# Latent attention heads: two banks in turn for the sums of values, and a ring of three banks for the rest

## The chip, the cores and the metric

One Trainium2 chip, one of its cores. The metric is the device time of the core in microseconds (us), median of several runs. The engines that matter here are TensorE (PE: matmuls, which write to PSUM alone), ScalarE (ACT), VectorE (DVE) and GpSimd (POOL). PSUM is the memory between them: 8 banks of 512 float32 values in each of 128 partitions.

## What is computed

Two layers of a hybrid backbone over 512 latent tokens and 256 context tokens, width 1024. Each layer has neighbourhood attention (4 heads), a bidirectional mLSTM (4 heads), latent attention (8 heads of 64 + 32 query and key features, 64 value features), an output projection for each, and a SwiGLU feed-forward part. The change lies in latent attention:

```python
def attend(q, k, v, scale):
    s = jnp.einsum('bqhd,bkhd->bhqk', q, k).astype(jnp.float32) * scale
    p = jax.nn.softmax(s, axis=-1).astype(v.dtype)
    return jnp.einsum('bhqk,bkhd->bqhd', p, v)

def mla_project(p, gq, gkv, w_uq, w_ukv, qk_gain, rope):
    B, T, _ = p[8].shape
    q = (rms_norm(p[8], gq) @ w_uq).reshape(B, T, MLA_HEADS, MLA_NOPE + MLA_ROPE)
    kv = (rms_norm(p[9], gkv) @ w_ukv).reshape(B, T, MLA_HEADS, MLA_NOPE + MLA_V)
    k_nope, v = kv[..., :MLA_NOPE], kv[..., MLA_NOPE:]
    k_rope = jnp.broadcast_to(p[10][:, :, None, :], (B, T, MLA_HEADS, MLA_ROPE))
    q = rms_norm(q, qk_gain[0])
    k = rms_norm(jnp.concatenate([k_nope, k_rope], axis=-1), qk_gain[1])
    if rope is not None:
        ...
    return q, k, v

# in each of the DEPTH layers, behind neighbourhood attention and the mLSTM:
qc_l, kc_l, vc_l = mla_project(pl, mla_gq[l], mla_gkv[l], w_uq[l], w_ukv[l], mla_qk_gain[l], rope)
qc_c, kc_c, vc_c = mla_project(pc, mla_gq[l], mla_gkv[l], w_uq[l], w_ukv[l], mla_qk_gain[l], None)
oc_l = blocked_attention(qc_l, jnp.concatenate([kc_l, kc_c], axis=1),
                         jnp.concatenate([vc_l, vc_c], axis=1), MLA_SCALE)
...
if need_ctx:
    oc_c = attend(qc_c, kc_c, vc_c, MLA_SCALE)
```

In layer 0 the context tokens are needed too (their queries attend to context keys alone); in layer 1, the last, they are keys and values but no queries.

## The kernel before, in words

Every engine runs its own hand-written program, and semaphores tie them together. Each float32 operand is split into a high part (fp32r) and a remainder, and a product is three matmuls (`mm3`, L877): high with high, high with low, low with high. GpSimd makes the low parts of the weights, which stream in by DMA from SyncE.

The latent heads of a layer are software-pipelined in `latent_pe` (L1224), `latent_act` (L692) and `latent_dve` (L1842). All three loop over h from -2 to 8, and inside over steps i (7 in layer 0, 6 in layer 1; `lat_steps`). While head h is scored, head h + 1 gets its scales, its rounded queries and keys and its column maxima, head h + 2 its projections, and head h - 1 its output. In one step TensorE runs, in this order:

- `scores(h, i)`: keys of tile i against all latent queries into a bank ("st"); step 6 of layer 0 is the context's own scores. ScalarE takes the exponential of it (L708) and so frees the bank; VectorE splits that into high part (L1864) and remainder (L1865).
- at i = 0, `q_sums`: sums of squares of the queries of h + 1 ("sumq"), read by ScalarE's Ln (L738).
- at i = 2, `k_project` of h + 2, then at i = 2 and 3 (in layer 0 once more at 5) `max_context`: scores of context keys for maxima ("ctx"), reduced by VectorE (L1901), at i = 3 `q_project` of h + 2; at i = 3, 4, 4, 5 `max_scores` ("max"), reduced by VectorE (L1896).
- at i = 4, `k_sums` of h + 2 ("sumk"), read by ScalarE's Ln (L729), which it does at i = 5, behind the exponential of step 5.
- `values` of the step two places back: values with a column of ones against the probabilities, summed over six steps in bank `AV_BANK` (7). In layer 0 a seventh step writes the context's sums into a ring bank ("avc").
- at the last step, `max_row` ("row"): the maxima of h + 1 turned into a row, which ScalarE copies (L754). Score step 0 of the next head waits for that copy.

The projections Q_PS and K_PS hold banks 3 to 5 (bank 4 is shared). Banks 0, 1, 2 and 6 form a ring: `ring_order` (L309) writes down the order of all fills of both layers once, and `fill` (L1228) has TensorE wait until the bank of fill number `at` was released by the reader of fill `at - 4`. A fill's reader is found with `filled`. Each fill is released by one instruction of ScalarE or VectorE.

The output of head h - 1 is made at step 2 of head h: ScalarE's `q_round` of h + 1, then `inverse(h - 1, 0)` (Ln L767, Exp L768) of the sums in `AV_BANK`, VectorE's product L1917 (`o_scale(h - 1, 0)`), then in layer 0 `inverse(h - 1, 1)`, which waits for L1917, and the product L1920 (`o_scale(h - 1, 1)`), whose drain releases "avc". Behind these VectorE has, in order, `k_rest` (L1887), `q_rest` (L1891), `probs_lo(h, 2)`, and at step 3 `max_c` twice (L1901), `o_rest` (L1928) and `probs_lo(h, 3)`. The first step of values of head h waits for L1917 of head h - 1, since both use `AV_BANK`:

```python
if i == 0 and o_count(l, h, 0):
    pe.wait_ge(o_mul, o_count(l, h, 0) - (1 if full and h else 0))
```

Names below: "st3" is the fill of score step 3, "ctx0" that of `max_context(h + 1, 0)`, "max0" of `max_scores(h + 1, 0)`, and so on. "Head 2" is the stretch from the start of score step 0 of h = 2 to that of h = 3.

Of the kernel before, what the change touches and what calls it, by code (L numbers as in the profile page):

```python
# [70 lines left out]
def build(nc, x_t, c_t, w_mod, w_stream, cols, rpb, c_f32, c_rope, c_gate, c_dir, out):  # L71
# [3 lines left out]
    with es:  # L75
# [268 lines left out]
            return (2 * h if l < DEPTH - 1 else MLA_HEADS * (DEPTH - 1) * 2 + h) + x  # L344

        RINGS = ring_order()
        RING_BANKS = (0, 1, 2, 6)
        K_PS = psum[:, 512 * 4 + 256:512 * 6]
        Q_PS = psum[:, 512 * 3:512 * 3 + TOK]
        AV_BANK = 7  # L350
        XQ, CQ = slice(0, SEQ), slice(SEQ, TOK)

        def o_rows(h):
# [97 lines left out]
        def _(act):  # L451
# [240 lines left out]
            def latent_act(l, full):  # L692
# [4 lines left out]

                def filled(*name):
                    at = RINGS[(l,) + name]
                    act.wait_ge(bank_full[at % 4], at // 4 + 1)  # L700
                    return bank(RING_BANKS[at % 4]), at % 4

                def probs(h, i):
                    s = lat_step(l, h, i)
# [19 lines left out]
                def k_rsqrt(h):  # L724
                    if G(h):
                        act.wait_ge(k_lo, G(h))
                    for x, (c0, c1) in enumerate(((CTX_LEN, TOK), (0, CTX_LEN))):
                        src, b = filled("sumk", h, x)
                        A(rk[:, c0:c1], src[:, 0:c1 - c0], ACT.Ln, bias=eps[:, 0:1], scale=1.0 / QK_DIM).then_inc(bank_free[b], 1)  # L729
                    act.wait_ge(bank_free[b], RINGS[l, "sumk", h, 1] // 4 + 1)  # L730
                    A(rk, rk, ACT.Exp, scale=-0.5).then_inc(k_r, 1)

                def q_rsqrt(h):
                    if G(h):
                        act.wait_ge(q_lo, G(h))
                    for x, cs in enumerate((XQ, CQ) if full else (XQ,)):
                        src, b = filled("sumq", h, x)
                        A(rq[:, cs], src[:, 0:cs.stop - cs.start], ACT.Ln, bias=eps[:, 0:1],  # L738
                          scale=1.0 / QK_DIM).then_inc(bank_free[b], 1)
                    act.wait_ge(bank_free[b], RINGS[l, "sumq", h, 1 if full else 0] // 4 + 1)  # L740
                    A(rq[:, 0:qw], rq[:, 0:qw], ACT.Exp, scale=-0.5).then_inc(q_r, 1)

                def k_round(h):
# [12 lines left out]
                def inverse(h, x):  # L756
                    ro, rs = o_rows(h)
                    cs = (XQ, CQ)[x]
                    if x == 0:
                        act.wait_ge(av_x, lat_x(l, h, TT - 1))  # L760
                        src = bank(AV_BANK)
                    else:
                        src, b = filled("avc", h)
                    m = o_count(l, h, x)
                    if m:
                        act.wait_ge(o_mul, m)
                    seq(A(MA["rec"][ro, cs], src[rs, 0:cs.stop - cs.start], ACT.Ln))  # L767
                    A(MA["rec"][ro, cs], MA["rec"][ro, cs], ACT.Exp, scale=-1.0).then_inc(o_rec, 1)  # L768
# [98 lines left out]
        def _(pe):  # L867
# [356 lines left out]
            def latent_pe(l, full):  # L1224
# [3 lines left out]
                def fill(*name):  # L1228
                    at = RINGS[(l,) + name]
                    assert at == nfill[0]  # L1230
                    nfill[0] += 1
                    if at >= 4:
                        pe.wait_ge(bank_free[at % 4], at // 4)
                    return bank(RING_BANKS[at % 4]), at % 4

                def scores(h, i):
                    dst, b = fill("st", h, i)
                    sl = h % 2
                    kh, kl, qh, ql = (MA[x][0:97, sl, :] for x in ("khi", "klo", "qhi", "qlo"))
                    if i == 0:  # L1240
                        pe.wait_ge(k_lo, G(h) + 1)
                        pe.wait_ge(q_lo, G(h) + 1)
                        at = RINGS[l, "row", h, 0]
                        pe.wait_ge(bank_free[at % 4], at // 4 + 1)
                    if i < TT:
                        ks = slice(P * i, P * i + P)
                        ins = mm3(dst, kh[:, ks], kl[:, ks], qh[:, XQ], ql[:, XQ], True, True)
                    else:
                        at = RINGS[l, "row", h, 1]
                        pe.wait_ge(bank_free[at % 4], at // 4 + 1)  # L1250
                        for k in range(CT):
                            ks = slice(P * k, P * k + P)
                            ins = mm3(dst[:, CTX_LEN * k:CTX_LEN * k + CTX_LEN], kh[:, ks], kl[:, ks],
                                      qh[:, CQ], ql[:, CQ], True, True)
                    ins.then_inc(bank_full[b], 1)

                def values(h, i):
                    s = lat_step(l, h, i)
                    pe.wait_ge(p_lo, s + 1)
                    if i < TT:  # L1260
                        if i == 0 and o_count(l, h, 0):
                            pe.wait_ge(o_mul, o_count(l, h, 0) - (1 if full and h else 0))
                        mm3(bank(AV_BANK), v_ones(hhi, h, i), v_ones(hlo, h, i), MA["phi"][:, s % 3, :],
                            MA["plo"][:, s % 3, :], i == 0, i == TT - 1).then_inc(av_x, 1)
                    else:
                        dst, b = fill("avc", h)
                        for k in range(CT):
                            cs = slice(CTX_LEN * k, CTX_LEN * k + CTX_LEN)
                            ins = mm3(dst[:, 0:CTX_LEN], v_ones(hhi, h, k), v_ones(hlo, h, k), MA["phi"][:, s % 3, cs],
                                      MA["plo"][:, s % 3, cs], k == 0, k == CT - 1)  # L1270
                        ins.then_inc(bank_full[b], 1)
# [190 lines left out]
        def _(dve):  # L1462
# [379 lines left out]
            def latent_dve(l, full):  # L1842
# [4 lines left out]

                def filled(*name):
                    at = RINGS[(l,) + name]
                    dve.wait_ge(bank_full[at % 4], at // 4 + 1)  # L1850
                    return bank(RING_BANKS[at % 4]), at % 4

                def probs_lo(h, i):
                    s = lat_step(l, h, i)
                    at = RINGS[l, "st", h, i]
                    dve.wait_ge(bank_free[at % 4], at // 4 + 1)
                    back = lat_back(l, h, i, 3)
                    if back is not None:
                        if back[1] < TT:
                            dve.wait_ge(av_x, lat_x(l, *back))  # L1860
                        else:
                            at = RINGS[l, "avc", back[0]]
                            dve.wait_ge(bank_full[at % 4], at // 4 + 1)
                    seq(V.tensor_copy(MA["phi"][:, s % 3, :], MA["p"][:, s % 2, :]))  # L1864
                    V.tensor_tensor(MA["plo"][:, s % 3, :], MA["p"][:, s % 2, :], MA["phi"][:, s % 3, :],  # L1865
                                    ALU.subtract).then_inc(p_lo, 1)

                def v_lo(t):
                    at = RINGS[l, "v", t]
                    dve.wait_ge(ma_v, TT * l + t + 1)  # L1870
                    v = bank(RING_BANKS[at % 4]).rearrange("p (j a n) -> p j a n", j=MLA_HEADS // 2, a=2)
                    V.tensor_tensor(v_heads(hlo, t, 0), v[:, :, 0, :], v_heads(hhi, t, 0), ALU.subtract)
                    V.tensor_tensor(v_heads(hlo, t, 1), v[:, :, 1, :], v_heads(hhi, t, 1), ALU.subtract).then_inc(bank_free[at % 4], 1)

                def k_scale(h):
                    dve.wait_ge(k_r, G(h) + 1)
# [26 lines left out]

                def max_both(h):
                    at = RINGS[l, "max", h, 3]
                    dve.wait_ge(bank_free[at % 4], at // 4 + 1)
                    V.tensor_tensor(mx[:, 8:12], mx[:, 0:4], mx[:, 4:8], ALU.max).then_inc(col_max, 1)

                def o_scale(h, x):
                    ro, rs = o_rows(h)  # L1910
                    cs = (XQ, CQ)[x]
                    m = o_count(l, h, x)
                    dve.wait_ge(o_rec, m + 1)
                    if x == 0:
                        if m:
                            dve.wait_ge(o_hi, m)
                        V.tensor_tensor(MA["of"][ro, cs], bank(AV_BANK)[ro, :], MA["rec"][ro, cs], ALU.mult).then_inc(o_mul, 1)  # L1917
                    else:
                        at = RINGS[l, "avc", h]
                        seq(V.tensor_tensor(MA["of"][ro, cs], bank(RING_BANKS[at % 4])[ro, 0:CTX_LEN], MA["rec"][ro, cs], ALU.mult))  # L1920
                        V.drain().then_inc(bank_free[at % 4], 1)
                        V.drain().then_inc(o_mul, 1)

                def o_rest(h, x):
# [285 lines left out]
```

## Time and profile before

| what | value |
|---|---|
| median of 3 runs | 2615.68 us (2615.37 to 2619.78) |
| the profiled execution, its time | 2617.63 us |
| the profiled execution, its span | 2615.9 us |
| mean granted clock of TensorE | 0.895 of full speed |
| latent heads of layer 0, first score to the end of the last head (640.97 to 853.00) | 212.0 us, TensorE busy 178.1 |
| latent heads of layer 1 (2029.88 to 2203.00) | 173.1 us, TensorE busy 139.4 |

The page gives busy time per engine, the chain of work that ended last and the costliest groups of instructions. A group's "idle before" says how long its engine had nothing to do ahead of it and what ended the idle time. Timelines list instructions by start; PE's matmuls are pipelined, so a busy TensorE isn't one at its peak, and successive rows overlap. The granted clock is the share of full speed that TensorE was allowed.

### The profile page before, as it was taken

What the parts mean: (1) busy time and instruction counts of PE and PEld (TensorE: products, weight loads), DVE (VectorE), ACT (ScalarE), POOL (GpSimd) and SP (SyncE); (2) the same over time, 40 slices, a digit from 0 to 9 for tenths busy, and PEclk for the clock granted to TensorE, in tenths of its full rate; (3) what the DMA queues carried; (4) which work ended last, traced back from release to release, by engine and by line L of the source; (5) the groups of instructions that cost most, each with busy time, mean ns of one, the idle gap of its engine ahead of it and who ended that gap; (6) DMA issues with size and microseconds to landing.
All of it is one profiled execution on the core that took longest, in us unless ns stands there. A gap on an engine that the chain in (4) does not pass through costs nothing.

```text
span 2615.9 us, 29223 instructions
## 1 busy us (share of the span) xinstructions
PE 2231.0 (85%) x11572; PEld 1781.0 (68%) x11572; DVE 1017.7 (39%) x1774; ACT 723.8 (28%) x1178; POOL 615.6 (24%) x820
## 2 busy tenths in 40 slices
PE   5777999596887799999999967798766887899998
PEld 4466766474665688788878855686655555688886
DVE  4457501616777511111201155550334885311211
ACT  3233222023554311111111133322113553322222
POOL 0110300021000233333333320031021101455555
PEclk8899965698998799999999979997588998999999
DMA  6200124010000124132323210021011000232322
GB/s 244 89 15 10 55 81 145 1 58 24 9 9 9 56 97 129 60 118 97 105 73 129 81 43 17 17 63 33 0 43 33 17 9 18 79 97 97 96 90 97
DMA packets 76733, 166.23 MB, mean 64 GB/s; under 512 B 5296, under 2 KB 47024, under 8 KB 75584
## 3 DMA queue, kind: packets, MB, share of 16 engines
q1 hardware_dynamic: 75648, 163.15, 19.1%
q8 instruction: 92, 1.51, 0.2%
q10 hardware_dynamic: 960, 1.31, 0.2%
q14 instruction: 33, 0.27, 0.0%
HBM read 162.33 MB, written 2.10 MB: 63 GB/s over the span
## 4 chain that ended last, share of the span: by engine, by line
PE 73%; DVE 13%; ACT 6%; issue 5%; DMA 1%; POOL 1%; SPq 0%; DVEq 0%; ACTq 0%; POOLq 0%
PE psum L879 19%; PE psum L880 18%; PE psum L881 18%; PE psum L1133 2%; PE psum L924 2%; PE psum L1158 2%; DMA wm<-w_mod 1%; PE psum L934 1%; PE psum L1121 1%; PE psum L1316 1%; DVE naptlo L1627 1%; PE psum L1176 1%; PE psum L1187 1%; DVE n_t L1536 1%; PE psum L1031 1%
## 5 line engine op out<-in xcount | busy, mean ns | idle before, releaser
L441 POOL TENSOR_TENSOR wlo<-raw,whi 128x256 fp32r<-128x256 f32 x816 | 615.4, 786 | 1987.4 <-ACT whi L467 1987.4
L879 PE MATMUL psum<-hhi,whi 128*128 128x512 f32 (+1 forms) x1640 | 587.4, 358 | 46.0 <-DVEq L1474 14.6
L880 PE MATMUL psum<-hlo,whi 128*128 128x512 f32 (+1 forms) x1640 | 582.0, 355 | 0.0
L881 PE MATMUL psum<-hhi,wlo 128*128 128x512 f32 (+1 forms) x1640 | 581.1, 354 | 0.0
L467 ACT ACTIVATE whi<-raw 128x1024 fp32r<-128x1024 f32 x204 | 215.3, 1059 | 1060.8 <-PE psum L881 1060.6
L879 PEld LDWEIGHTS psum<-hhi,whi 128*128 128x128 f32 x1640 | 314.2, 192 | 102.2 <-issue 21.8
L881 PEld LDWEIGHTS psum<-hhi,wlo 128*128 128x128 f32 x1640 | 314.2, 192 | 42.7
L880 PEld LDWEIGHTS psum<-hlo,whi 128*128 128x128 f32 x1640 | 314.8, 192 | 40.6
L1983 DVE TENSOR_TENSOR ffuf<-ffsa,psum 128x768 f32<-128x768 f32 (+1 forms) x44 | 36.1, 821 | 534.2 <-ACT ffsa L828 534.2
L879 PE MATMUL psum<-uhi,whi 128*128 128x512 f32 (+1 forms) x528 | 190.9, 362 | 8.3 <-POOL wlo L441 7.5
L880 PE MATMUL psum<-ulo,whi 128*128 128x512 f32 (+1 forms) x528 | 189.6, 359 | 0.0
L881 PE MATMUL psum<-uhi,wlo 128*128 128x512 f32 (+1 forms) x528 | 189.3, 359 | 0.0
L1991 DVE SCALAR_TENSOR_TENSOR xres<-psum,mods,xres 128x512 f32<-128x512 f32 x72 | 45.4, 659 | 262.5 <-PE psum L881 262.5
L879 PEld LDWEIGHTS psum<-uhi,whi 128*128 128x128 f32 x528 | 100.0, 189 | 26.9 <-POOL wlo L441 9.2
L880 PEld LDWEIGHTS psum<-ulo,whi 128*128 128x128 f32 x528 | 100.6, 191 | 16.0
L881 PEld LDWEIGHTS psum<-uhi,wlo 128*128 128x128 f32 x528 | 100.0, 189 | 16.3
L1721 DVE TENSOR_TENSOR mle<-mle,psum 128x768 f32<-128x768 f32 x16 | 15.3, 955 | 228.3 <-ACT mle L648 172.2
L708 ACT ACTIVATE map<-psum 128x512 f32<-128x512 f32 x104 | 61.7, 595 | 136.8 <-PE psum L881 135.7
L1865 DVE TENSOR_TENSOR maplo<-map,maphi 128x512 fp32r<-128x512 f32 x104 | 75.4, 725 | 3.6
L879 PE MATMUL psum<-maphi,hhi 128*128 128x512 f32 (+1 forms) x112 | 53.7, 479 | 25.7 <-DVE maof L1917 24.1
L1553 DVE SCALAR_TENSOR_TENSOR xres<-psum,mods,xres 128x512 f32<-128x512 f32 x72 | 45.4, 659 | 70.2 <-PE psum L881 70.2
L924 PE MATMUL psum<-wm,csil 128*32 128x256 f32 x768 | 64.8, 465 | 3.3 <-DMA wm<-w_mod 3.3
(280 smaller groups left out, 3443.0 us busy)
## 6 DMA issues: line engine op xcount, KB each, us to landing
raw<-w_stream SPq DMA_DIRECT2D x204, 512.0 KB, 3.5
wm<-w_mod SPq DMA_DIRECT2D x80, 512.0 KB, 4.6
wm<-w_mod SPq DMA_DIRECT2D x8, 1024.0 KB, 17.3
xres<-x_t SPq DMA_DIRECT2D x8, 384.0 KB, 6.0
out<-xres SPq DMA_DIRECT2D x8, 256.0 KB, 2.9
mlsel<-c_gate ACTq DMA_DIRECT2D x2, 216.0 KB
consts<-c_f SPq DMA_DIRECT2D x1, 353.0 KB, 7.1
marope<-c_rope ACTq DMA_DIRECT2D x4, 64.0 KB
```

The source lines that it names most:

```text
L441: ins = nc.gpsimd.tensor_tensor(wlo[:, q % 2, c:c + UW // 4], raw[:, q % RAW, c:c + UW // 4], whi[:, q % 2, c:c + UW // 4], ALU.subtract)
L467: A(whi[:, q % 2, :], raw[:, q % RAW, :], ACT.Copy).then_inc(hi_done, 1)
L708: A(MA["p"][:, s % 2, :], src, ACT.Exp, scale=scale).then_inc(bank_free[b], 1)
L879: mm(dst, ah, bh, start=first, stop=False)
L880: mm(dst, ah, bl, start=False, stop=False)
L881: return mm(dst, al, bh, start=False, stop=last)
L924: ins = mm(dst[32 * j:32 * j + 32, 0:256], csil[:, 4 * half + j, :], w[:, j, :], start=half == 0, stop=half == 1)
L1133: mm(dst, sel[:, P * x:P * x + P], rows[:, 2, r0:r1], start=True, stop=False)
L1158: ins = mm(bank(4 + d)[:, 65 * c:65 * c + 65], e[:, d, P * c:P * c + P], va[:, c, h, :], start=True, stop=True)
L1553: ins = V.scalar_tensor_tensor(xres[:, m, r0:r1], psum_pair(psum, m % 4)[:, r0:r1], mods[:, l, 16 + m, cls(r0):cls(r0) + 1], xres[:, m, r0 ...
L1865: V.tensor_tensor(MA["plo"][:, s % 3, :], MA["p"][:, s % 2, :], MA["phi"][:, s % 3, :], ALU.subtract).then_inc(p_lo, 1)
L1991: ins = V.scalar_tensor_tensor(xres[:, m, r0:r1], psum_pair(psum, m % 2)[:, r0:r1], mods[:, l, 40 + m, cls(r0):cls(r0) + 1], xres[:, m, r0 ...
```

## The change

Bank 6 leaves the ring and becomes a second bank for the sums of values; even heads use bank 7, odd heads bank 6. The first step of values of head h waits for the product L1917 of head h - 2 instead of h - 1 (in layer 1 the heads 0 and 1 wait for the last output of layer 0). The ring has three banks: fill `at` waits for the release of fill `at - 3`. Every other place that named the ring's 4 names its length. The order of instructions on every engine is the same; line numbers behind L346 grow by one.

```diff
         RINGS = ring_order()
-        RING_BANKS = (0, 1, 2, 6)
+        RING_BANKS = (0, 1, 2)
+        NRB = len(RING_BANKS)
         K_PS = psum[:, 512 * 4 + 256:512 * 6]
         Q_PS = psum[:, 512 * 3:512 * 3 + TOK]
-        AV_BANK = 7
+        AV_BANKS = (7, 6)
...
                 def filled(*name):
                     at = RINGS[(l,) + name]
-                    act.wait_ge(bank_full[at % 4], at // 4 + 1)
-                    return bank(RING_BANKS[at % 4]), at % 4
+                    act.wait_ge(bank_full[at % NRB], at // NRB + 1)
+                    return bank(RING_BANKS[at % NRB]), at % NRB
...
                     if x == 0:
                         act.wait_ge(av_x, lat_x(l, h, TT - 1))
-                        src = bank(AV_BANK)
+                        src = bank(AV_BANKS[h % 2])
...
                     at = RINGS[(l,) + name]
                     assert at == nfill[0]
                     nfill[0] += 1
-                    if at >= 4:
-                        pe.wait_ge(bank_free[at % 4], at // 4)
-                    return bank(RING_BANKS[at % 4]), at % 4
+                    if at >= NRB:
+                        pe.wait_ge(bank_free[at % NRB], at // NRB)
+                    return bank(RING_BANKS[at % NRB]), at % NRB
...
                     if i < TT:
-                        if i == 0 and o_count(l, h, 0):
-                            pe.wait_ge(o_mul, o_count(l, h, 0) - (1 if full and h else 0))
-                        mm3(bank(AV_BANK), v_ones(hhi, h, i), v_ones(hlo, h, i), MA["phi"][:, s % 3, :],
+                        if i == 0 and (l or h >= 2):
+                            pe.wait_ge(o_mul, o_count(l, h - 2, 0) + 1 if h >= 2 else o_count(l, 0, 0))
+                        mm3(bank(AV_BANKS[h % 2]), v_ones(hhi, h, i), v_ones(hlo, h, i), MA["phi"][:, s % 3, :],
                             MA["plo"][:, s % 3, :], i == 0, i == TT - 1).then_inc(av_x, 1)
...
-                        V.tensor_tensor(MA["of"][ro, cs], bank(AV_BANK)[ro, :], MA["rec"][ro, cs], ALU.mult).then_inc(o_mul, 1)
+                        V.tensor_tensor(MA["of"][ro, cs], bank(AV_BANKS[h % 2])[ro, :], MA["rec"][ro, cs], ALU.mult).then_inc(o_mul, 1)
                     else:
                         at = RINGS[l, "avc", h]
-                        seq(V.tensor_tensor(MA["of"][ro, cs], bank(RING_BANKS[at % 4])[ro, 0:CTX_LEN], MA["rec"][ro, cs], ALU.mult))
-                        V.drain().then_inc(bank_free[at % 4], 1)
+                        seq(V.tensor_tensor(MA["of"][ro, cs], bank(RING_BANKS[at % NRB])[ro, 0:CTX_LEN], MA["rec"][ro, cs], ALU.mult))
+                        V.drain().then_inc(bank_free[at % NRB], 1)
                         V.drain().then_inc(o_mul, 1)
```

Left out: the same replacement of 4 by NRB in the other waits on bank_full and bank_free (ScalarE's Ln and Exp, TensorE's waits of `scores` for "row", VectorE's `filled`, `probs_lo`, `v_lo` and `max_both`), which wait for the same events as before.

## Rows read from the trace of the kernel before

**Rows 1.** The page, part 1: busy us, share of the span, instructions of each engine

```profile
PE 2231.0 (85%) x11572; PEld 1781.0 (68%) x11572; DVE 1017.7 (39%) x1774; ACT 723.8 (28%) x1178; POOL 615.6 (24%) x820
```

**Rows 2.** Waits of TensorE over the span: us in total, times, longest

```profile
PE psum L879 <- DVE maof L1917: 24.1, 14, 2.8
```

**Rows 3.** Stretches: one head each, then half-clock and full-clock ones; columns in the head row

```profile
core 0: us, PE busy (x) PEld busy (x) DVE busy (x) ACT busy (x) POOL busy (x), PEclk, DMA share, GB/s
693.50:720.62 27.12, 23.70 (x109) 17.35 (x109) 21.60 (x35) 15.80 (x27) 3.45 (x4) 0.94 0.06 19
2072.11:2094.17 22.06, 18.08 (x80) 12.74 (x80) 18.96 (x30) 12.60 (x20) 3.55 (x4) 1.00 0.08 25
2094.17:2117.03 22.86, 19.66 (x79) 14.00 (x80) 17.98 (x30) 11.57 (x20) 0.00 (x0) 0.93 0.00 1
703.68:707.09 3.41, 3.41 (x10) 2.74 (x11) 2.52 (x4) 1.35 (x4) 0.00 (x0) 0.50 0.00 0
707.10:710.80 3.70, 3.70 (x22) 3.19 (x21) 3.56 (x7) 1.14 (x2) 0.00 (x0) 1.00 0.00 0
```

**Rows 4.** Timeline, layer 0, head 2: start, duration, engine, line, operation [idle before]

```profile
703.53 0.63 PE L879 MATMUL psum<-maphi,hhi 128*128 128x512 f32 x1 [1.57 <-DVE maof L1917]
...
704.33 0.43 DVE L1920 TENSOR_TENSOR maof<-psum,marec 64x256 f32<-64x256 f32 x1 [0.95 <-ACT marec L768]
...
704.81 0.63 PE L879 MATMUL psum<-maqhi,makhi 97*128 97x512 f32 x1
...
706.51 0.63 PE L1327 MATMUL psum<-makhi,maqhi 96*128 96x512 f32 x1
...
707.91 1.29 DVE L1901 TENSOR_REDUCE mamax<-psum 128x2 f32<-128x512 f32 x2
...
710.84 0.40 PE L879 MATMUL psum<-maqhi,makhi 97*128 97x512 f32 x1
```

**Rows 5.** Timeline, the same head, from its score step 4 on

```profile
711.75 0.60 ACT L708 ACTIVATE map<-psum 128x512 f32<-128x512 f32 x1 [3.48 <-PE psum L881]
...
712.01 1.45 PE L1316 MATMUL psum<-masqk,consts 96*128 96x512 f32 x4
...
714.00 0.40 PE L879 MATMUL psum<-maqhi,makhi 97*128 97x512 f32 x1
...
715.02 0.68 DVE L1896 TENSOR_REDUCE mamax<-psum 128x1 f32<-128x512 f32 x1
715.52 1.05 ACT L729 ACTIVATE mar<-psum,eps 128x512 f32<-128x512 f32 x2
...
715.76 0.50 PE L1327 MATMUL psum<-makhi,maqhi 96*128 96x512 f32 x1 [0.89 <-DVE mamax L1896]
...
716.26 0.50 PE L1337 MATMUL psum<-makhi,maqhi 96*128 96x256 f32 x2
```

**Rows 6.** Timeline, layer 1: head 2 in two lines, then head 3

```profile
2083.16 0.39 PE L1327 MATMUL psum<-makhi,maqhi 96*128 96x512 f32 x1
...
2083.99 1.29 DVE L1901 TENSOR_REDUCE mamax<-psum 128x2 f32<-128x512 f32 x2
...
2105.45 0.68 DVE L1901 TENSOR_REDUCE mamax<-psum 128x2 f32<-128x512 f32 x1
...
2106.27 0.53 PE L1327 MATMUL psum<-makhi,maqhi 96*128 96x512 f32 x1
...
2113.66 0.40 PE L1327 MATMUL psum<-makhi,maqhi 96*128 96x512 f32 x1
...
2114.36 1.05 ACT L729 ACTIVATE mar<-psum,eps 128x512 f32<-128x512 f32 x2
...
2115.13 1.03 PE L1346 MATMUL psum<-consts,mamax 128*1 128x128 f32 x8 [0.37 <-ACT mar L729]
```

**Rows 7.** Timeline, layer 0, head 7, the last of the layer

```profile
834.50 0.42 DVE L1920 TENSOR_TENSOR maof<-psum,marec 64x256 f32<-64x256 f32 x1 [0.95 <-ACT marec L768]
...
837.67 0.63 PE L879 MATMUL psum<-maqhi,makhi 97*128 97x512 f32 x1
```

More of the change, by code:

```diff
@@ L729, in k_rsqrt @@
                         A(rk[:, c0:c1], src[:, 0:c1 - c0], ACT.Ln, bias=eps[:, 0:1], scale=1.0 / QK_DIM).then_inc(bank_free[b], 1)
-                    act.wait_ge(bank_free[b], RINGS[l, "sumk", h, 1] // 4 + 1)
+                    act.wait_ge(bank_free[b], RINGS[l, "sumk", h, 1] // NRB + 1)
                     A(rk, rk, ACT.Exp, scale=-0.5).then_inc(k_r, 1)
@@ L739, in q_rsqrt @@
                           scale=1.0 / QK_DIM).then_inc(bank_free[b], 1)
-                    act.wait_ge(bank_free[b], RINGS[l, "sumq", h, 1 if full else 0] // 4 + 1)
+                    act.wait_ge(bank_free[b], RINGS[l, "sumq", h, 1 if full else 0] // NRB + 1)
                     A(rq[:, 0:qw], rq[:, 0:qw], ACT.Exp, scale=-0.5).then_inc(q_r, 1)
@@ L1243, in scores @@
                         at = RINGS[l, "row", h, 0]
-                        pe.wait_ge(bank_free[at % 4], at // 4 + 1)
+                        pe.wait_ge(bank_free[at % NRB], at // NRB + 1)
                     if i < TT:
@@ L1249, in scores @@
                         at = RINGS[l, "row", h, 1]
-                        pe.wait_ge(bank_free[at % 4], at // 4 + 1)
+                        pe.wait_ge(bank_free[at % NRB], at // NRB + 1)
                         for k in range(CT):
@@ L1849, in filled @@
                     at = RINGS[(l,) + name]
-                    dve.wait_ge(bank_full[at % 4], at // 4 + 1)
-                    return bank(RING_BANKS[at % 4]), at % 4
+                    dve.wait_ge(bank_full[at % NRB], at // NRB + 1)
+                    return bank(RING_BANKS[at % NRB]), at % NRB
                 def probs_lo(h, i):
@@ L1855, in probs_lo @@
                     at = RINGS[l, "st", h, i]
-                    dve.wait_ge(bank_free[at % 4], at // 4 + 1)
+                    dve.wait_ge(bank_free[at % NRB], at // NRB + 1)
                     back = lat_back(l, h, i, 3)
@@ L1862, in probs_lo @@
                             at = RINGS[l, "avc", back[0]]
-                            dve.wait_ge(bank_full[at % 4], at // 4 + 1)
+                            dve.wait_ge(bank_full[at % NRB], at // NRB + 1)
                     seq(V.tensor_copy(MA["phi"][:, s % 3, :], MA["p"][:, s % 2, :]))
@@ L1870, in v_lo @@
                     dve.wait_ge(ma_v, TT * l + t + 1)
-                    v = bank(RING_BANKS[at % 4]).rearrange("p (j a n) -> p j a n", j=MLA_HEADS // 2, a=2)
+                    v = bank(RING_BANKS[at % NRB]).rearrange("p (j a n) -> p j a n", j=MLA_HEADS // 2, a=2)
                     V.tensor_tensor(v_heads(hlo, t, 0), v[:, :, 0, :], v_heads(hhi, t, 0), ALU.subtract)
-                    V.tensor_tensor(v_heads(hlo, t, 1), v[:, :, 1, :], v_heads(hhi, t, 1), ALU.subtract).then_inc(bank_free[at % 4], 1)
+                    V.tensor_tensor(v_heads(hlo, t, 1), v[:, :, 1, :], v_heads(hhi, t, 1), ALU.subtract).then_inc(bank_free[at % NRB], 1)
                 def k_scale(h):
@@ L1905, in max_both @@
                     at = RINGS[l, "max", h, 3]
-                    dve.wait_ge(bank_free[at % 4], at // 4 + 1)
+                    dve.wait_ge(bank_free[at % NRB], at // NRB + 1)
                     V.tensor_tensor(mx[:, 8:12], mx[:, 0:4], mx[:, 4:8], ALU.max).then_inc(col_max, 1)
```

## The prediction

> **What bounds the kernel now.** The page first: TensorE is busy 85% of the span, no other engine half as much [rows 1], so the question is where TensorE waits. The list of its waits has one entry that this change aims at: 14 waits, 24.1 us together, for the product of L1917, which frees the bank that holds the sums of values [rows 2]. They are the first step of values of heads 1 to 7 in both layers. Then the stretches: a head takes 27.1 us in layer 0 and about 22 to 23 in layer 1, and TensorE is idle 3 to 4 us of it [rows 3]; VectorE is busy 18 to 22 us, so it has its own order of work that TensorE can run into. The timelines of single heads show what TensorE finds when it asks for a bank [rows 4 to 7]. The clock belongs to it: the granted clock is 0.94 in the layer 0 head, 1.00 and 0.93 in two heads of layer 1; its low level is 0.50, 1.2 GHz instead of 2.4, for 3.41 us behind the wait for L1917 [rows 3]. A matmul of 512 columns lasts 0.63 us in it and 0.40 outside [rows 4].
>
> **How I read the ring.** The order of the fills is the same in both kernels, no instruction is added, and none changes place. What changes is that fill number n waits for the release of fill n-3, not n-4. In layer 0 a head makes 21 fills, which in order are: st0, sumq0, sumq1, st1, avc (of the head before), st2, ctx0, st3, ctx1, max0, st4, max1, max2, sumk0, sumk1, st5, max3, ctx2, st6, row0, row1. In layer 1 the same without sumq1, avc, ctx2, st6 and row1. So for each fill I take the release of the one three places ahead from the timeline and set it beside the start of the fill in the kernel before. Where the release is earlier, the third bank costs nothing; the row of the other engine is the cover. Where it is later, TensorE is late by the difference, if that release doesn't hang on something that moves too.
>
> **Layer 0, head 2.** The first step of values waited 1.57 us for L1917 [rows 4]. With its own bank it starts about 1.6 us sooner. Behind it stands st3, which now waits for avc, and avc is released by the later product of L1920: 704.33 + 0.43 = 704.76, against a start of st3 at 704.81 [rows 4]. So the wait moves one step on and is as long: gain nothing.
> Then max0 waits for ctx0, whose reduction is the first of the pair at 707.91, done at about 708.56; max0 was at 706.51 [rows 4]. VectorE gets there after its products, two remainders and a remainder of the probabilities, none of which waits for the values. TensorE is 2.1 us late at st4. Everything behind max0 (the query projection of the head after next, values, st4) is queued behind this wait; before, max0 to st4 took 4.33 us.
> sumk0 now waits for the exponential of st4: 711.75 + 0.60 = 712.35 against 712.01 [rows 5], 0.4 with the signal. It is hidden in the next one: st5 waits for max2, reduced until 715.02 + 0.68 = 715.70, against 714.00 [rows 5]. That reduction hangs on st4 (exponential, rounding of the output, remainders, reduction), so it moves with st4 and the difference of 1.7 is added.
> max3 waits for sumk0, whose Ln is the first of two from 715.52 to 716.57: about 716.2 against 715.76; ctx2 waits for sumk1: 716.57 against 716.26 [rows 5]. That adds 0.4. The other fills find their bank free, or (st6, row0, row1) wait for other things already.
> Sum: 2.1 + 1.7 + 0.4 = **4.2 us late per head**. Five heads (1 to 5) have all of it: 21. Head 0 has no avc and no late products: 1. Head 6 makes no sumk and no projection: 1.5. Head 7 gains: it has no maxima, st4 waits for avc, 834.50 + 0.42 = 834.92, instead of following at 837.67 [rows 7], so 2.5 sooner. Layer 0: **+21**.
>
> **Layer 1, heads 2 and 3.** There is no avc, so here the values' own bank does free st3, by the whole wait. But max0 meets ctx0: in head 3 its reduction ends at 2105.45 + 0.68 = 2106.13, and max0 was at 2106.27: the gain is lost to the new wait, net 0. In head 2 it ends at about 2084.64 and max0 was at 2083.16: 1.5 late [rows 6]. sumk0 waits 0.4 for st4's exponential as in layer 0, and nothing absorbs it. max3 waits for the first Ln of the pair at 2114.36, done at about 2115.05, against 2113.66 [rows 6]: 1.4 late, and the row of maxima, which needs max3's reduction and stood at 2115.13, is late by the same. So 1.9 in a head like 3 and 3.0 to 3.3 in one like 2; with two of the first and three of the second kind, +13 for heads 1 to 5. Head 0: +3. Head 6: +1. Head 7, where only the wait for L1917 is left and goes: -3. Layer 1: **+14**.
>
> **The clock.** The traces show no head with these longer stops, so this is bounded. Now one idle stretch of 1.6 us in a head is followed by 3.41 us at the low level, mostly [rows 3, 4]; in layer 1's head 2 it is not [rows 3]. Changed, a full head stops some 2.2 us twice ahead of max0, and again near st5 and max3. A slow stretch with work all through it costs half its length, 1.7 us. Least: no more of them, 0. Most: two more in each of 13 full heads, 44 us. I take one more in 10 or 11 of the 13, **18 us**, since the stops next to the known one are longer than it is.
>
> **Sum.** 21 + 14 + 18 = +53 us on the profiled execution's 2617.6 gives 2670.6. That execution lies 1.9 us above the median of the three runs, so against the median I say **2668.7 us**, 2.0% slower.
>
> **The rivals.**
> Faster. The added bank takes away the 24.1 us [rows 2] and the ring waits stay hidden, since VectorE and ScalarE run ahead once TensorE comes sooner: 2615.7 - 24.1 = 2591.6. It decides at max0: if ctx0 is reduced before TensorE asks (within 0.45 us of st3's end), this holds. For it speaks the length of the wait. Against it, the reduction stands on VectorE behind L1917 and L1920 themselves, which is why I give it 0.05. The Trainium skill (Perfetto Trace Analysis, Matmuls) says independent groups should rotate through different banks so that emptying one overlaps the next; applied to the values alone it gives this time, applied to the ring it speaks against the change.
> No change. The new waits replace idle time that each head had anyway, as at max0 in layer 1's head 3, everywhere: 2616. That needs the differences at st5 and max3 to vanish: 0.04. The Trainium skill (TensorE: Matmul & The Clock Gate, HAM oscillation) tells of a kernel in which a second PSUM buffer gave no further gain; no run here shows such a case yet.
> Ring waits without the clock. The stops fall so that the low level covers only idle time: 2615.7 + 35 = 2650.7, chance 0.25.
> Two more slow stretches per head: 2615.7 + 35 + 44 = 2694.7, chance 0.16.
> My forecast has 0.50.
>
> **How the numbers follow.** The range goes from 2638, the rival without clock if each of 13 heads also wins back 1 us because VectorE starts sooner, to 2697, just past the rival with two slow stretches. About 0.2% (5 us) is what a measurement of this kernel can tell from no change. Faster 0.05; same 0.04; slower 0.91.
>
> **What would show it.** In the profile of the changed kernel the waits for L1917 are gone or nearly so; in layer 0 st3 waits for L1920 (7 times, about 2 us); max0 waits for the reduction of L1901's line (12 to 14 times, 2 us in layer 0); st5 waits for the reduction of L1896's line in layer 0, max3 for the Ln of L729's line in both. Heads of 31 to 34 us in layer 0 and 24 to 28 in layer 1, the last head of each layer shorter by 2 to 3, all other stages alike. The forecast is wrong if max0 isn't late, that is, if VectorE's remainders run before the point where I have them; or if the clock stays at 0.93 and above in these heads, which leaves 2651.

## The result and the profile after

The changed kernel takes 2675.03 us (median of 4 runs, 2672.64 to 2678.07) against 2615.52 for the kernel before: a ratio of 1.0225 with a 95% interval of 1.0213 to 1.0238. It is 2.25% slower; forecast were 2668.7 us, 2638 to 2697. One of the four executions of ring3_av2_best below took 4318.3 us; it is left out of that kernel's median and ratio.

The page's line of busy time, which answers to [rows 1]: every engine but TensorE did the same work in the same time; TensorE shows 26 us more for the same 11572 matmuls, in line with a lower granted clock (0.886 over the span against 0.895).

```profile
PE 2256.7 (84%) x11572; PEld 1791.3 (67%) x11572; DVE 1016.5 (38%) x1774; ACT 723.7 (27%) x1178; POOL 614.7 (23%) x820
```

The spans differ by 60.4 us (2676.3 against 2615.9). From the first score to the last matmul on values the latent heads of layer 0 took 244.0 us instead of 204.4 (+39.6), those of layer 1 187.8 instead of 169.5 (+18.3), the two stretches ahead of them, in which no head is scored yet, +2.2 and +0.6. All other stages agree within 2 us.

The waits of TensorE (line waited at, releaser: us in all, times, longest). Lines are one higher than in the kernel before.

```profile
PE psum L1328 <- DVE mamax L1902: 30.9, 14, 3.2
...
PE psum L1328 <- ACT mar L730: 15.7, 12, 1.4
PE psum L880 <- DVEq L1922: 14.7, 7, 2.5
...
PE psum L1323 <- ACT mar L730: 4.7, 2, 2.4
PE psum L880 <- DVE mamax L1897: 4.5, 5, 1.0
...
PE psum L1317 <- ACT map L709: 3.8, 12, 0.3
```

No wait for L1918, the old L1917, is left of the 24.1 us of [rows 2]. In its place stand 30.9 us at max0 and its like for the reduction of the context scores (L1902), 15.7 us at max3 for the Ln of the key sums (L730), 14.7 us at st3 for the release of avc (L1922, the drain behind L1921), 4.5 us for reductions of L1897, st5's, and 3.8 us at sumk0 for the exponential of st4 (L709). Each was an entry of the forecast. The 4.7 us at L1323 are not: they were 0.9 us before.

Layer 0, head 2, in the changed kernel (timeline; the head starts at 707.38; this answers to [rows 4, 5]):

```profile
715.68 0.39 PE L880 MATMUL psum<-maphi,hhi 128*128 128x512 f32 x1
...
718.22 0.43 DVE L1921 TENSOR_TENSOR maof<-psum,marec 64x256 f32<-64x256 f32 x1 [0.94 <-ACT marec L769]
...
718.76 0.50 PE L880 MATMUL psum<-maqhi,makhi 97*128 97x512 f32 x1 [2.21 <-DVEq L1922]
...
721.80 1.29 DVE L1902 TENSOR_REDUCE mamax<-psum 128x2 f32<-128x512 f32 x2
...
722.55 0.79 PE L1328 MATMUL psum<-makhi,maqhi 96*128 96x512 f32 x1 [2.04 <-DVE mamax L1902]
...
728.25 0.40 PE L880 MATMUL psum<-maqhi,makhi 97*128 97x512 f32 x1
...
732.42 0.68 DVE L1897 TENSOR_REDUCE mamax<-psum 128x1 f32<-128x512 f32 x1
...
733.16 0.50 PE L880 MATMUL psum<-maqhi,makhi 97*128 97x512 f32 x1 [1.04 <-DVE mamax L1897]
...
734.79 1.05 ACT L730 ACTIVATE mar<-psum,eps 128x512 f32<-128x512 f32 x2
...
735.53 0.50 PE L1328 MATMUL psum<-makhi,maqhi 96*128 96x512 f32 x1 [1.40 <-ACT mar L730]
```

The first matmul on values now starts at 715.68, with no wait. st3 waits 2.21 us for avc and starts 11.4 us into the head, 11.3 before. max0 starts 15.2 us into the head instead of 13.0, right behind the first of the two reductions. st4 stands at 20.9 instead of 17.3, st5 4.9 us behind st4 instead of 3.2, max3 2.4 behind st5 instead of 1.8. Behind st3's stop, from 719.2 to 726.0, most of TensorE's matmuls of 512 columns last 0.63 us; at st4, 728.25, they last 0.40 again.

Layer 1, head 1, start at 2098.04 (answers to [rows 6]):

```profile
2105.28 0.40 PE L880 MATMUL psum<-maphi,hhi 128*128 128x512 f32 x1
...
2105.98 0.40 PE L880 MATMUL psum<-maqhi,makhi 97*128 97x512 f32 x1
...
2109.32 1.28 DVE L1902 TENSOR_REDUCE mamax<-psum 128x2 f32<-128x512 f32 x2
...
2110.05 0.50 PE L1328 MATMUL psum<-makhi,maqhi 96*128 96x512 f32 x1 [2.97 <-DVE mamax L1902]
...
2118.65 1.05 ACT L730 ACTIVATE mar<-psum,eps 128x512 f32<-128x512 f32 x2
...
2119.38 0.50 PE L1328 MATMUL psum<-makhi,maqhi 96*128 96x512 f32 x1 [1.26 <-ACT mar L730]
```

Here the second bank does what it is for up to st3, which starts 7.9 us into the head. Then TensorE stands 2.97 us at max0, and 1.26 at max3.

Single heads and one stretch, with the granted clock (PEclk), for [rows 3]:

```profile
core 0: us, PE busy (x) PEld busy (x) DVE busy (x) ACT busy (x) POOL busy (x), PEclk, DMA share, GB/s
707.38:741.78 34.40, 26.44 (x109) 18.74 (x109) 21.59 (x35) 15.79 (x27) 3.45 (x4) 0.85 0.05 15
2122.76:2149.31 26.55, 19.90 (x80) 13.82 (x80) 18.81 (x30) 12.60 (x20) 3.46 (x4) 0.94 0.07 20
2098.04:2122.76 24.72, 18.68 (x80) 12.59 (x80) 17.72 (x30) 11.57 (x20) 0.00 (x0) 1.00 0.00 0
719.20:726.00 6.80, 4.76 (x13) 3.60 (x12) 6.24 (x10) 1.91 (x3) 0.00 (x0) 0.50 0.00 0
```

Layer 0's head 2 takes 34.4 us instead of 27.1, at 0.85 instead of 0.94; 6.8 us in one piece are at the low level. Layer 1's head 2 takes 26.6 instead of 22.1, at 0.94 instead of 1.00; its head 1, at 1.00, 24.7.

### The profile page after: what moved, and what is told of

It is laid out like the page before. It is cut to its first block, busy times and chain, and to the rows that moved or that the text cites. A ratio compares the mean times of both kernels' runs of the same rounds, so it can differ in the third digit from the quotient of the medians.

```text
span 2676.3 us, 29223 instructions
## 1 busy us (share of the span) xinstructions
PE 2256.7 (84%) x11572; PEld 1791.3 (67%) x11572; DVE 1016.5 (38%) x1774; ACT 723.7 (27%) x1178; POOL 614.7 (23%) x820
## 4 chain that ended last, share of the span: by engine, by line
PE 72%; DVE 14%; ACT 7%; issue 6%; DMA 1%; POOL 1%; SPq 0%; DVEq 0%; ACTq 0%; POOLq 0%
PE psum L880 19%; PE psum L881 18%; PE psum L882 18%; PE psum L1134 2%; PE psum L925 2%; PE psum L1159 2%; DMA wm<-w_mod 1%; PE psum L935 1%; PE psum L1122 1%; PE psum L1328 1%; DVE naptlo L1628 1%; PE psum L1177 1%; PE psum L1188 1%; PE psum L1347 1%; DVE n_t L1537 1%
## 5 line engine op out<-in xcount | busy, mean ns | idle before, releaser
L709 ACT ACTIVATE map<-psum 128x512 f32<-128x512 f32 x104 | 61.6, 594 | 185.9 <-PE psum L882 183.4
L1897 DVE TENSOR_REDUCE mamax<-psum 128x1 f32<-128x512 f32 x64 | 43.8, 687 | 87.0 <-PE psum L1328 86.9
L880 PE MATMUL psum<-maqhi,makhi 97*128 97x512 f32 (+1 forms) x112 | 49.5, 442 | 28.0 <-DVEq L1922 14.7
```

The lines of the kernel that those rows point to most:

```text
L709: A(MA["p"][:, s % 2, :], src, ACT.Exp, scale=scale).then_inc(bank_free[b], 1)
L880: mm(dst, ah, bh, start=first, stop=False)
```

## The experiments

Each kernel is compared with the kernel before, measured beside it (its medians were 2615.5 to 2619.8 us). "Heads" are the stretches from the first score to the last matmul on values, in the profiled execution: before 204.4 and 169.5 us, changed 244.0 and 187.8.

| kernel | ring | banks for values | median us | ratio to before (95%) | heads, layer 0 and 1, us |
|---|---|---|---|---|---|
| the change | 3 | 2 | 2675.0 | 1.0225 (1.0213 to 1.0238) | 244.0, 187.8 |
| ring3_av1 | 3 | 1 | 2678.8 | 1.0238 (1.0221 to 1.0255) | 241.9, 185.8 |
| ring3_av2_busy | 3 | 2 | 2670.1 | 1.0200 (1.0183 to 1.0218) | 240.2, 186.4 |
| ring3_av2_max2 | 3 | 2 | 2664.6 | 1.0178 (1.0160 to 1.0196) | 231.8, 185.6 |
| ring3_av2_ln | 3 | 2 | 2654.9 | 1.0133 (1.0116 to 1.0150) | 228.5, 181.9 |
| ring3_av2_ctx | 3 | 2 | 2654.4 | 1.0139 (1.0115 to 1.0162) | 228.4, 180.0 |
| ring3_av2_all | 3 | 2 | 2607.2 | 0.9951 (0.9934 to 0.9968) | 199.4, 159.9 |
| ring3_av2_best | 3 | 2 | 2588.1 | 0.9866 (0.9846 to 0.9886) | 180.7, 155.9 |
| ring4_ctx | 4 | 1 | 2615.2 | 0.9995 (0.9984 to 1.0006) | 202.4, 169.4 |
| ring4_all | 4 | 1 | 2609.7 | 0.9969 (0.9956 to 0.9981) | 197.6, 166.3 |
| ring4_inv | 4 | 1 | 2598.6 | 0.9924 (0.9905 to 0.9944) | 196.3, 157.7 |
| ring4_inv1 | 4 | 1 | 2586.8 | 0.9874 (0.9857 to 0.9891) | 188.0, 156.6 |
| ring4_inv1_ln | 4 | 1 | 2581.4 | 0.9856 (0.9840 to 0.9873) | 178.2, 154.0 |

### ring3_av1: the ring's loss alone

```diff
-        AV_BANKS = (7, 6)
+        AV_BANKS = (7, 7)
...
-                        if i == 0 and (l or h >= 2):
-                            pe.wait_ge(o_mul, o_count(l, h - 2, 0) + 1 if h >= 2 else o_count(l, 0, 0))
+                        if i == 0 and o_count(l, h, 0):
+                            pe.wait_ge(o_mul, o_count(l, h, 0) - (1 if full and h else 0))
```

> The change with one bank for the sums of values again (bank 7), the ring still of three, bank 6 unused. Theory (the ring's third bank costs the time, and the second bank for values gives almost nothing because its gain ends at the next ring wait): 2675 to 2690 us, layer 0's heads 34 to 34.5 us as in the change, the wait for L1917 back with 20 to 24 us, the last head of layer 1 longer by 5. Rival (the second bank is worth its 24 us and the ring costs 84): 2695 to 2700 us.

2678.8 us, 3.8 more than the change. The intervals of the two ratios overlap widely, so that no gain by the second bank is shown, and a gain of 24 us is ruled out; in the profiled executions the heads are even 4 us shorter with one bank. The waits show where the 24 us go:

```profile
PE psum L880 <- DVE maof L1918: 23.8, 14, 2.8
...
PE psum L1328 <- DVE mamax L1902: 17.9, 11, 2.1
PE psum L1328 <- ACT mar L730: 15.7, 12, 1.4
...
PE psum L880 <- DVEq L1922: 2.3, 5, 0.7
```

With one bank TensorE waits 23.8 us for L1918 and then 17.9 at max0 and 2.3 for avc; with two it waits none for L1918, but 30.9 and 14.7. The first set sums to 44.0, the second to 45.6. In layer 1, head 1 (start at 2096.39), st3 comes 9.8 us into the head instead of 7.9, and max0 at 12.0 in both. The last head of layer 1 takes 15.5 us instead of 12.3, that of layer 0, however, 16.0 instead of 18.1:

```profile
2106.14 0.39 PE L880 MATMUL psum<-maqhi,makhi 97*128 97x512 f32 x1
...
2108.41 0.50 PE L1328 MATMUL psum<-makhi,maqhi 96*128 96x512 f32 x1 [1.19 <-DVE mamax L1902]
```

### ring3_av2_ctx and ring4_ctx: ctx0 released early

```diff
                         if i == 2:
+                            if nxt:
+                                max_c(h + 1, 0)
                             if was:
                                 o_scale(h - 1, 0)
...
                             if nxt:
-                                max_c(h + 1, 0)
                                 max_c(h + 1, 1)
```

> The change with VectorE's reduction of ctx0 moved ahead of the output products and remainders of step 2. Theory (max0 stands behind ctx0's late release, and the low clock behind that stop costs as well): the 31 us of waits for L1901's line fall under 5 us, heads of layer 0 from 34.4 to 30 to 32 us, of layer 1 to 21.5 to 23.5 us, 2630 us in all (2618 to 2645). Rival (VectorE is the bound and another wait takes the place at once): 2665 us or more.

> Control: the same move of ctx0's reduction in the kernel before, with its ring of four. Theory: max0 doesn't wait for ctx0 there, so no gain, 2612 to 2618 us. Rival (the move helps by itself, for instance because the reductions are ready sooner for the row of maxima): under 2605 us.

The order alone is worth nothing with four banks (2615.2, ratio 0.9995) and 21 us with three. The lateness at max0 is real and belongs to the ring. But 2630 us were expected and 2645 at most: the gain is half of what was forecast, and the waits say in part why:

```profile
PE psum L1328 <- ACT mar L730: 15.7, 12, 1.4
PE psum L880 <- DVEq L1922: 15.1, 7, 2.5
...
PE psum L1328 <- DVE mamax L1897: 9.7, 7, 2.0
```

The 30.9 us for L1902 are gone. At L1328, now at max2, stand 9.7 us for the reduction of max0 (L1897), which VectorE makes behind the remainders of step 3: TensorE got there sooner, and that release was next. The wait for avc and the one at max3 stayed as they were. The clock has a part too: in the heads of layer 1 the mean granted clock is 0.88 (the change: 0.93), and these heads take 23.5 to 26.9 us where 21.5 to 23.5 were expected.

### ring3_av2_max2 and ring3_av2_ln: the releases of max2 and sumk0

```diff
                             if nxt:
                                 max_x(h + 1, 0)
                                 max_x(h + 1, 1)
+                                max_x(h + 1, 2)
...
                         if i == 5 and nxt:
-                            max_x(h + 1, 2)
                             max_x(h + 1, 3)
```

> The change with VectorE's reduction of max2 moved from step 5 to step 4, ahead of the output's remainder and the remainder of the probabilities. Theory (in layer 0 st5 waits for max2's release, 1.5 to 1.8 us in each of five heads): 7 us and up to as much again from the clock, 2664 us (2655 to 2669), all of it in layer 0. Rival (that stop only moves, since st5 and what follows are bound by other engines): 2672 us or more.

2664.6 us; the gain is 12 us in the heads of layer 0 and 2 in those of layer 1, and the 4.5 us of waits at st5 are gone. That is as forecast, in the time and in the layer.

```diff
                     for i in range(n):
+                        if now and i == 5 and nxt2:
+                            k_rsqrt(h + 2)
                         if now:
                             probs(h, i)
...
-                        if i == 5 and nxt2:
+                        if i == 5 and nxt2 and not now:
                             k_rsqrt(h + 2)
```

> The change with ScalarE's Ln of the key sums ahead of the exponential of step 5, alone. Theory: max3 no longer waits for the release of sumk0 (15.7 us over 12 waits in the change), in layer 1 1.4 us a head with what the clock adds, in layer 0 0.4: 2655 us (2645 to 2664). Rival (the exponential that is made later takes it back): 2670 us or more.

2654.9 us, as forecast in sum, but not in its parts: in the profiled executions 15.5 us come from layer 0 and 5.9 from layer 1, where I had expected the larger part. The forecast counted the difference to the kernel before in layer 0, 0.4 us; this move takes the whole wait away, about 1.4 us [the stop of 1.40 at 735.53 above], the 0.9 that the kernel before had there included [rows 5]. That is 7 us for five heads. The rest fits the clock: 0.88 instead of 0.85 over the heads of layer 0 is 18 us less at the low level, worth up to 9 us of work.

### ring3_av2_all and ring4_all: the three moves together

> The change with three moves of readers: ctx0's reduction ahead of the output products (as in ring3_av2_ctx), max2's reduction at step 4, and ScalarE's Ln of the key sums ahead of the exponential of step 5, so that max3 isn't late. Theory (the loss is the lateness of single readers, each of which can be taken away): 2632 us (2615 to 2645), the waits for L729's line under 4 us outside the prologue. Rival (with three banks a full head always runs into one of them, whatever the readers' order): 2650 us or more.

> The kernel before (ring of four, one bank for the sums of values) with the three moves of readers of ring3_av2_all. It tells how much of ring3_av2_all's 2607 us comes from the readers' order alone. Theory (the moves take away mostly what the ring of three had added, in the kernel before only its waits of 0.9 and 0.3 us at max3 and ctx2): 2605 us (2598 to 2612). Rival (the moves are worth the same in both): under 2590 us.

With three banks the moves together give 68 us, more than their single gains (21 + 10 + 20), with four banks 9 us. For three banks 2632 us were forecast, and 2615 at least; that was 25 us too high. The loss thus hangs on the readers' order: with the same order a ring of three and two banks for values (2607.2) and a ring of four with one (2609.7) are equal within their intervals. The ring's lost bank still costs something, however. ring4_all still waits 24.6 us for the old L1917 (L1919 there), ring3_av2_all not at all, but it waits 15.6 us for avc and 9.6 for the reductions of maxima in their place. So the second bank for values only balances the ring's remaining waits. The surplus of the three moves over their single gains, 17 us, fits the clock: by the mean granted clock, the heads of both layers have about 100 us at the low level in the change, 98, 84 and 88 with the moves of ctx0, max2 and the Ln alone, and 38 with all three, and each microsecond less is worth up to half of one. That is an estimate from the rounded clock, and no run separates it. The heads of ring3_av2_all, one row a layer:

```profile
core 0: us, PE busy (x), PEclk, DMA share, GB/s
645.90:845.33 199.43, 168.82 (x770) 0.93 0.04 11
2031.83:2191.74 159.91, 134.35 (x564) 0.97 0.04 14
```

In the changed kernel it is lower, 0.85 and 0.93:

```profile
core 0: us, PE busy (x), PEclk, DMA share, GB/s
644.93:888.95 244.02, 190.43 (x770) 0.85 0.03 9
2073.13:2260.97 187.84, 144.15 (x564) 0.93 0.04 12
```

### ring3_av2_busy: the clock by itself

Five matmuls of 512 columns more ahead of max0 in heads 1 to 6, into the bank of values that is free then. Their results are read by nobody.

```diff
-                    now, nxt, nxt2 = (0 <= x < MLA_HEADS for x in (h, h + 1, h + 2))
+                    now, nxt, nxt2, was = (0 <= x < MLA_HEADS for x in (h, h + 1, h + 2, h - 1))
...
+                        if nxt and was and now and i == 3:
+                            pe.wait_ge(o_mul, o_count(l, h - 1, 0) + 1)
+                            for _ in range(5):
+                                mm(bank(AV_BANKS[(h + 1) % 2]), MA["qhi"][0:96, (h + 1) % 2, 0:P],
+                                   MA["khi"][0:96, (h + 1) % 2, CTX_LEN:TOK], start=True, stop=True)
                         if nxt and i == 3:
                             max_scores(h + 1, 0)
```

> The change with five matmuls of 512 columns more ahead of max0 in heads 1 to 6 of both layers, into the bank of the next head's sums of values, which nobody reads: TensorE is busy in the stop where it waits for ctx0. Theory (the low clock behind that stop costs some 1.3 to 1.7 us a head): 2660 us (2652 to 2669) and a higher granted clock in the heads, at the same time of max0 within its head. Rival (the clock has no part in the loss, the matmuls only come on top): 2675 us or more.

2670.1 us, between the two theories and short of both; the interval of its ratio just overlaps that of the change. In layer 0, head 2, the added matmuls fill the stop, at the low level (five take 2.29 us), and max0 comes as late as in the change, 15.2 us into the head:

```profile
712.90 0.63 PE L1338 MATMUL psum<-makhi,maqhi 96*128 96x256 f32 x2
...
713.33 2.29 PE L1368 MATMUL psum<-makhi,maqhi 96*128 96x512 f32 x5
...
715.49 0.50 PE L1328 MATMUL psum<-makhi,maqhi 96*128 96x512 f32 x1
```

Here the low stretch ended with them, after 3.6 us instead of 6.8, and the head took 31.3 us instead of 34.4. So keeping TensorE busy there can give 3 us back. But of the heads 1 to 5 it was the only one; the others stayed at 34.1 to 34.5 (in head 3, with the same stop filled, the matmuls behind max0 still last 0.63 us), and the clock of the stage hardly rose:

```profile
638.00:878.15 240.15, 196.62 (x800) 0.86 0.03 9
2062.63:2249.06 186.43, 149.92 (x594) 0.95 0.04 12
```

The level had fallen before them, as the 0.63 us of the row at 712.90 show; they don't fill the stop at st3. The experiment shows in one head that the clock has a part in the loss; how large it is over all heads is not shown, nor why the level came back in this head alone.

### ring4_inv, ring4_inv1, ring4_inv1_ln, ring3_av2_best: the wait for L1917 without a bank

ring4_inv puts ScalarE's inverse ahead of the rounding of the queries, for which ScalarE waits anyway; ring4_inv1 makes inverse and product at step 1. The edit of ring4_inv1:

```diff
+                        if i == 1 and was:
+                            inverse(h - 1, 0)
                         if i == 2:
                             if nxt:
                                 q_round(h + 1)
-                            if was:
-                                inverse(h - 1, 0)
-                                if full:
-                                    inverse(h - 1, 1)
+                            if was and full:
+                                inverse(h - 1, 1)
...
-                        if i == 1 and nxt:
-                            q_scale(h + 1)
-                        if i == 2:
+                        if i == 1:
+                            if nxt:
+                                q_scale(h + 1)
                             if was:
                                 o_scale(h - 1, 0)
-                                if full:
-                                    o_scale(h - 1, 1)
+                        if i == 2:
+                            if was and full:
+                                o_scale(h - 1, 1)
```

> The kernel before with ScalarE's inverse of the latent sums moved ahead of the rounding of the queries, so that L1917 comes earlier and the one bank is free when the next head's values come. It takes the wait of 24.1 us away without a bank from the ring. Theory: 24 us and part of the low clock behind those waits, 2585 us (2575 to 2594), waits for L1917 under 5 us. Rival (the gain ends at the next wait, as it did in the change): 2608 us or more.

> The kernel before (ring of four, one bank for the sums of values) with ScalarE's inverse of the latent sums and VectorE's product L1917 made at step 1 instead of step 2. Theory: the 12.7 us that ring4_inv still waits for L1917 fall under 3, 2588 us (2580 to 2594). Rival (the next wait takes the rest): 2598 us, as ring4_inv.

ring4_inv: 2598.6 us, a smaller gain than expected (2594 at most were forecast), with 12.7 us of the wait left, 2.8 at the most in one head (the row's last number), which is what the last heads had before:

```profile
PE psum L879 <- DVE maof L1917: 12.7, 14, 2.8
```

ring4_inv1: 2586.8 us. The wait is down to 2.8 us, and the next ones are those of the ring:

```profile
PE psum L1316 <- DVE mamax L1896: 7.4, 10, 1.5
...
PE psum L1337 <- ACT mar L729: 5.1, 6, 1.1
...
PE psum L879 <- DVE maof L1917: 2.8, 2, 1.5
```

> ring4_inv1 with the Ln of the key sums ahead of the exponential of step 5, so that ctx2 in layer 0 and the row in layer 1 don't wait for it (5.1 and 2.4 us in ring4_inv1). Theory: 2579 us (2573 to 2585). Rival (ScalarE's later exponential takes it back): 2587 us as ring4_inv1.

> The change with all moves: the inverse and L1917's product at step 1, the other product, then ctx0's reduction ahead of the remainders, max2's reduction at step 4, the Ln of the key sums ahead of the exponential of step 5. Theory (layer 0's st3 waits for avc no more, 2.3 us in each of six heads, and with that the low clock goes): 2590 us (2580 to 2600). Rival (the ring of three keeps it above 2600 us).

ring4_inv1_ln, with the Ln of the key sums ahead of the exponential of step 5, has the lowest median of the study, 2581.4 us, 1.4% under the kernel before. Its heads run at 0.99 and 0.98:

```profile
core 0: us, PE busy (x), PEclk, DMA share, GB/s
642.55:820.71 178.16, 159.50 (x770) 0.99 0.04 13
2005.68:2159.64 153.96, 132.64 (x564) 0.98 0.04 14
```

ring3_av2_best, the change with all moves (the product of the context's sums, then ctx0's reduction, ahead of the remainders), takes 2588.1. The intervals of the two ratios overlap, so that the one is better than the other is not shown. It may be that once the product is early the second bank for values has little left to give; no run tests that with all else equal.

## Why the prediction was right, step by step

- **The wait for L1917.** Forecast: gone, and worth nothing in layer 0 because st3 meets avc, worth nothing at max0 in layer 1. So it is: st3 at 11.4 us into the head against 11.3, max0 of layer 1 at 12.0. ring3_av1 shows it directly.
- **max0.** Forecast 2.1 us in layer 0's head 2; 15.2 against 13.0 us into the head is 2.2.
- **st5 and max3, layer 0.** Forecast 1.7 and 0.4: st5 is 1.75 us further from st4, and max3 0.6 us further from st5. With these the ring costs 4.5 us in the head, forecast 4.2. The head lost 7.3 us; the other 2.8 are the clock, seen as 3.5 us of lateness at st4 where max0 was only 2.2 late, and 1.4 more between max3 and the next head. In both places the matmuls last 0.63 us, where they lasted 0.40 before.
- **Layer 1.** Forecast 1.9 us in heads like 3, 3.0 to 3.3 in heads like 2, clock apart. Head 1 lost 1.9 (24.7 against 22.8). Its clock is 1.00 now and was 0.93, but that gives nothing: the work that the low stretch had slowed stands ahead of max0, and max0 waits for ctx0's release all the same. Head 2 lost 4.5. Max0 is 1.5 us later in it and max3 1.6 further from st5 (forecast 1.5 and 1.4); 1.6 more lie between max0 and st4 and are the clock's, which fell from 1.00 to 0.94 in this head.
- **The ends.** Heads 7 were forecast 2.5 and 3 us shorter. In layer 0 st4 does come 2.6 us sooner in the head (7.9 us against 10.5), but the head is no shorter (18.1 against 18.2): TensorE waits 0.9 us for remainders of the probabilities behind st4, and the low level, the same in sum (0.81), now lies over the work behind that. In layer 1 it was 5.7, because the slow stretches went as well (clock 1.00, before 0.72). The two errors cancel, and that is luck. The changed kernel's last heads:

```profile
870.81:888.95 18.14, 14.89 (x57) 0.81 0.00 1
2248.72:2260.97 12.25, 11.10 (x42) 1.00 0.01 2
```

- **What the sum left out.** The sums of the first head's queries wait for the Ln of its key sums now: 4.7 us at L1323 instead of 0.9, in the stretches ahead of the heads, where I had put nothing. These stretches are 2.8 us longer in sum.
- **The clock.** Forecast 18 us, from one slow stretch more in 10 or 11 of 13 heads. In layer 0 the granted clock fell from 0.92 to 0.85 over the heads, 40 us more at the low level, up to 20 us of work. If the ring costs each of heads 1 to 5 the 4.5 us of head 2, 2.1 to 2.8 us in each are left for the clock. In layer 1 it stayed at 0.93: heads 1, 3 and 7 gained what the others lost. So the size of 18 us fits, though no run isolates it; its place was wrong, since nearly all is in layer 0. That the sum over both layers comes near the forecast, though neither layer does, is luck as well.

The signs named in advance came, with three exceptions: the full heads of layer 0 take 34.0 to 34.5 us, where 31 to 34 were given; only one of the two last heads is shorter; and in layer 1 the granted clock over the heads stayed at 0.93, which was named as a sign of being wrong, while in layer 0 it fell to 0.85. The forecast of 53 us against 60 measured in the span is short by the prologue, the fuller clock loss of layer 0 and head 0 of each layer (2.8 and 5.5 us instead of 1 and 3).

## What to carry to other kernels

A bank moved from a shared ring to one user takes away that user's wait and makes every fill of the ring one release more urgent; read the release of fill n - 3 against the start of fill n, one by one, before the change, and the places and sizes of the new waits are there; what the clock adds is not. A wait that goes is worth only the distance to the next late release, and several late releases taken away together gave 68 us where singly they gave 51. Before a bank is spent on a wait, look whether the release can come earlier: one ScalarE pair and one VectorE product moved by a step gave 1.3% with no bank at all.

## What had not been expected

Stops that are moved and split cost clock besides time: in layer 0's head 2 the ring's lateness came to 4.5 us and the low level to 2.8 more. Filling one of the two stops with matmuls gave 3 us back in head 2 alone, although the level had already fallen ahead of them. And a stop that goes does not always bring the clock back: with ctx0 released early, 18.1 us of stops at max0 in layer 1 became 8.0 at max2, and the granted clock of its heads fell from 0.93 to 0.88.
